# Feed-forward low parts moved from GpSimd to VectorE, adaLN halves replanned, bias copies spread: a two-layer hybrid diffusion backbone in float32

## The reference, cut to what matters

```python
for i in range(2):
    ml = adaln_terms(c[:, None, :], ada_w[i], ada_b[i])      # 9 terms of 1024: silu(c) @ ada_w + ada_b
    mc = adaln_terms(c_ctx, ada_w[i], ada_b[i])
    h = h + 0.5 * ml[2] * swiglu(modulate(h, norm_g[i, 0], ml[0], ml[1]), ffn_w_up[i, 0], ffn_w_down[i, 0])
    u = modulate(h, norm_g[i, 1], ml[3], ml[4])
    y = mixer(u)                                             # ends in an output projection
    h = h + ml[5] * y
    h = h + 0.5 * ml[8] * swiglu(modulate(h, norm_g[i, 2], ml[6], ml[7]), ffn_w_up[i, 1], ffn_w_down[i, 1])
    # hc (context) likewise, except that it is not needed after layer 1's mixer
return rmsnorm(h, final_norm_g)
```

## Time and profile before

| | before |
|---|---|
| median of 3 executions | 3018.96 us (3016.99 to 3019.55) |
| the profiled execution, its own time | 3020.68 us |
| its span, first to last instruction | 3018.9 us |
| PE busy | 2851.4 us (94%) |
| PE weight loads busy | 2653.7 us (88%) |
| DVE busy | 2255.8 us (75%) |
| ACT busy | 1255.2 us (42%) |
| POOL busy | 645.8 us (21%) |
| granted PE clock, mean | 0.984 of full |

### The profile page before, as it was taken

The page is one execution under the profiler, slowest core; times in us unless marked ns, Lnnn a source line. Parts: engine busy times, 40 slices in busy tenths (PEclk is TensorE's granted clock), DMA queues, the critical chain, the costliest instruction groups (busy, mean ns, idle before and its releaser), DMA issues.

```text
span 3018.9 us, 48480 instructions
## 1 busy us (share of the span) xinstructions
PE 2851.4 (94%) x18175; PEld 2653.7 (88%) x18175; DVE 2255.8 (75%) x3813; ACT 1255.2 (42%) x2458; POOL 645.8 (21%) x508
## 2 busy tenths in 40 slices
PE   8699999999999998988999999999999989999998
PEld 8689988999988886888999999889999877888887
DVE  7988888885546657398877787888888456498676
ACT  4234323543454456323433354333334336535444
POOL 1211011133332215221011113101111234431112
PEclk9899999999999999999999999999999999999999
DMA  6234444323320022232333322243332210223332
GB/s 251 85 100 130 117 131 137 90 80 119 127 79 15 8 75 79 70 104 68 104 116 126 116 88 64 64 132 123 132 126 82 89 36 2 78 72 103 98 88 81
DMA packets 160965, 285.49 MB, mean 95 GB/s; under 512 B 44078, under 2 KB 65502, under 8 KB 160606
## 3 DMA queue, kind: packets, MB, share of 16 engines
q1 hardware_dynamic: 157998, 275.99, 29.1%
q10 hardware_dynamic: 2736, 6.40, 0.5%
HBM read 270.73 MB, written 15.10 MB: 95 GB/s over the span
## 4 chain that ended last, share of the span: by engine, by line
PE 70%; DVE 16%; issue 5%; ACT 4%; SPq 2%; DMA 1%; POOL 1%; DVEq 0%; ACTq 0%; POOLq 0%
PE psum L2307 33%; PE psum L2322 26%; DVE ada_product L2005 2%; PE psum L2529 2%; DVE stats L1812 1%; SPq L999 1%; PE psum L2612 1%; DVE o_acc L2136 1%; DVE held L1812 1%; PE psum L2635 1%; DVE h L2266 1%; DVE wl L1788 1%; PE psum L2622 1%; PE psum L2514 1%; DVE sq L1694 1%
## 5 line engine op out<-in xcount | busy, mean ns | idle before, releaser
L1153 POOL TENSOR_TENSOR wl<-raw,wh 128x512 fp32r<-128x512 f32 (+3 forms) x278 | 477.8, 1719 | 2018.0 <-ACT wh L1247 2011.0
L1247 ACT ACTIVATE wh<-raw 128x512 fp32r<-128x512 f32 (+2 forms) x713 | 462.3, 665 | 556.6 <-DVE raw L1768 295.3
L2307 PE MATMUL psum<-uh,wh 128*128 128x256 f32 (+5 forms) x1552 | 399.8, 339 | 32.4 <-DVE h L2266 11.6
L2307 PE MATMUL psum<-uh,wl 128*128 128x256 f32 (+5 forms) x1552 | 395.5, 336 | 0.0
L2307 PE MATMUL psum<-ul,wh 128*128 128x256 f32 (+5 forms) x1552 | 395.1, 336 | 0.0
L2005 DVE SCALAR_TENSOR_TENSOR ada_product<-ada_w,cb 128x1024 f32<-128x1024 f32 x256 | 346.2, 1352 | 21.7 <-DMA ada_w<-in_ada_w 14.4
L2266 DVE SCALAR_TENSOR_TENSOR h<-psum,mod,h 128x512 f32<-128x512 f32 x360 | 215.0, 632 | 191.7 <-PE psum L2307 191.3
L2307 PE MATMUL psum<-ah,wh 128*128 128x512 f32 (+4 forms) x1040 | 304.6, 356 | 46.7 <-DVE h L2266 15.7
L1788 DVE TENSOR_TENSOR wl<-raw,wh 128x512 fp32r<-128x512 f32 x432 | 300.9, 697 | 51.3 <-ACT wh L1247 45.7
L2307 PEld LDWEIGHTS psum<-uh,wh 128*128 128x128 f32 (+1 forms) x1552 | 257.0, 190 | 59.2 <-DVE h L2266 14.7
L2307 PE MATMUL psum<-al,wh 128*128 128x512 f32 (+4 forms) x1040 | 298.3, 350 | 0.0
(11 more groups left out here) (324 smaller groups left out, 5137.2 us busy)
## 6 DMA issues: line engine op xcount, KB each, us to landing
raw<-in_w SPq DMA_DIRECT2D x448, 256.0 KB, 2.7
ada_w<-in_ada_w SPq DMA_DIRECT2D x128, 512.0 KB, 3.8
raw<-in_w SPq DMA_DIRECT2D x88, 512.0 KB, 3.7
spill<-cacc ACTq DMA_DIRECT2D x16, 384.0 KB, 2.4
scale_w<-in_scale_w SPq DMA_DIRECT2D x8, 512.0 KB, 14.6
raw<-in_w SPq DMA_DIRECT2D x32, 128.0 KB, 2.4
ada_w<-bias_final SPq DMA_DIRECT2D x16, 256.0 KB, 3.1
ada_start<-in_ada_w SPq DMA_DIRECT2D x7, 512.0 KB, 15.7
```

Source lines behind the costliest of these rows:

```text
L1153: nc.gpsimd.tensor_tensor(weight_tile(x, wl), raw_tile(slot_of[x]), weight_tile(x, wh).bitcast(f32), ALU.subtract).then_inc(lo_split, 1)
L1247: nc.scalar.activation(weight_tile(x, wh), src, ACT.Copy).then_inc(hi_split, 1)
L2307: ins = nc.tensor.matmul(bank, wt[:, k * w:(k + 1) * w], xt[:, k, cols], start=first, stop=last)
```

## The change

Four things change.

1. DVE makes the low parts of all gate, up and down units except the first three of (0,0), and those of the output projections' items 2 to 7, in `weight_lows(i)`, which takes the place of `pair_lows(i)` and goes through all its units in product order. POOL keeps the low parts of proj and of items 0 and 1 of each output projection.
2. The plan: term 8 of each layer goes over the eight items of the output projection before block 2. The first part of (0,1) has none any more. In later parts the downs of part 1 (two chunks) have no share; 84 shares carry 80 halves in (0,0) and 64 in (0,1) and (1,0).
3. SP issues two bias copies at each quarter product and each down from chunk 10's P1 on, instead of eight at P1 and P2.
4. At the first item of an output projection SP waits until the attention's maxima are done (unit 15 in layer 0, the last unit, 55, in layer 1) before it goes on to that item's loads; and the masks' load waits for the halves planned before it instead of for all.

The rest (`parts_of`, `classic_part`, `makes`, `t_made`, `u_made`) rewrites constants as functions with the same values. The diff, cut:

```diff
+def classic_part(x):
+    return 0
+def classic_pairs(x):
+    return sum(parts_of(x)[:classic_part(x) + 1])
...
     def shares(x):
         if x[0] == "down":
-            return 2 if x[3] + 1 < len(PARTS) else 0
+            full = x[3] + 1 < len(PARTS) and parts_of(x)[x[3]] == HALF_K
+            return 2 if full and x[3] != classic_part(x) else 0
+        if x[3] <= classic_part(x):
+            return 1 if x[3] else 0
         return {"P7": 1, "P5": 1}.get(x[0], 0)
...
+    def outs(layer):
+        return [i for i, x in enumerate(items) if x[:2] == ("out", layer)]
     over(ahead_of_downs(0, 0)[FUSED:], ada_chunks(0, [2]))
-    over(later_parts(0, 0), ada_chunks(0, range(3, 8)))
-    over(ahead_of_downs(0, 1), ada_chunks(0, [8]))
-    over(later_parts(0, 1), ada_chunks(1, range(4)))
-    over(later_parts(1, 0), ada_chunks(1, range(4, N_MOD)))
+    over(spread_out(0, 0), ada_chunks(0, range(3, 8)))
+    over(outs(0), ada_chunks(0, [8]))
+    over(spread_out(0, 1), ada_chunks(1, range(4)))
+    over(spread_out(1, 0), ada_chunks(1, range(4, 8)))
+    over(outs(1), ada_chunks(1, [8]))
...
+    vector_lows = [x for x, _, _, _ in units[FUSED:] if x[0] in ("gate", "up", "down") + PAIR or (x[0] == "out" and x[2] >= 2)]
...
             for x in items:
+                if x[:1] + x[2:] == ("out", 0):
+                    sp.wait_ge(max_done, 2 * (16 if x[1] == 0 else 56))
                 load_ada(number[x] if x[0] == "norm" and norm_no[x] else number[x] - ADA_LAG)
...
-                    elif windows and x[5] >= 10:
-                        if x[5] == 10 and not second:
-                            sp.wait_ge(table_made, 16 * 16)
-                        for wnd in windows[:8]:
-                            window(*wnd)
-                        windows = windows[8:]
+                    elif x[5] == 10 and not second:
+                        sp.wait_ge(table_made, 16 * 16)
+                        windows_due = windows
+                if x[0] in PAIR + ("down",) and x[1:3] == (0, 0):
+                    for wnd in windows_due[:2]:
+                        window(*wnd)
+                    windows_due = windows_due[2:]
...
-                    sp.wait_ge(ada_summed, on_dve(len(ada_order)))
+                    sp.wait_ge(ada_summed, on_dve(ADA_FIRST + sum(not v for i, c in plan.items() if i < number[x] for _, v in c)))
...
                     x, n, _, _ = units[done[0]]
-                    if x in low_no:
+                    if x not in vector_lows:
                         pool.wait_ge(lo_split, low_no[x])
...
-            def pair_lows(i):
-                while low_done[0] < len(pair_units) and issued(unit_of[pair_units[low_done[0]]], i):
-                    x = pair_units[low_done[0]]
-                    for y in sums_ahead.get(low_done[0], []):
+            def weight_lows(i):
+                while low_done[0] < len(vector_lows) and issued(unit_of[vector_lows[low_done[0]]], i):
+                    x = vector_lows[low_done[0]]
+                    for y in sums_ahead.get(x, []):
                         quarter_sum(y)
+                    if x in low_no:
+                        dve.wait_ge(lo_split, low_no[x])
                     dve.wait_ge(hi_split, unit_of[x] + 1)
-                    nc.vector.tensor_tensor(weight_tile(x, wl), pair_weight(x), weight_tile(x, wh).bitcast(f32),
-                                            ALU.subtract).then_inc(pair_lo, 1)
+                    src, done = (raw_tile(slot_of[x]), lo_split) if x in low_no else (pair_weight(x), pair_lo)
+                    nc.vector.tensor_tensor(weight_tile(x, wl), src, weight_tile(x, wh).bitcast(f32),
+                                            ALU.subtract).then_inc(done, 1)
```

More of the change, by code:

```diff
@@ L15 @@
 PARTS = [4, 2, 4, 4, 4, 4]
-CLASSIC = 4
+FIRST_PARTS = PARTS
 HALF_K = KD // 2
 QUARTER = HALF_K * P
-T_STEPS = 7 * HALF_K
 EPS = 1e-6
@@ L52, in segments, with parts_of @@
     return [LAT] if (layer, f) == (DEPTH - 1, 1) else [LAT, CTX]
+def parts_of(x):
+    return FIRST_PARTS if x[1:3] == (0, 0) else PARTS
+def classic_part(x):
+    return 0
+def classic_pairs(x):
+    return sum(parts_of(x)[:classic_part(x) + 1])
 def ffn_products(layer, f):
     items = []
-    chunks = [(layer, f, part, c, sum(PARTS[:part]) + c) for part, n in enumerate(PARTS) for c in range(n)]
-    for part, n in enumerate(PARTS):
+    parts, classic = (of(("", layer, f)) for of in (parts_of, classic_pairs))
+    chunks = [(layer, f, part, c, sum(parts[:part]) + c) for part, n in enumerate(parts) for c in range(n)]
+    for part, n in enumerate(parts):
         for key in [x for x in chunks if x[2] == part]:
             j = key[-1]
-            if j < CLASSIC:
+            if j < classic:
                 items += [("gate",) + key, ("up",) + key]
                 continue
-            if j == CLASSIC:
+            if j == classic:
                 items += [("P1",) + key, ("P2",) + key]
@@ L91, in shares, with within, spread_out @@
         if x[0] == "down":
-            return 2 if x[3] + 1 < len(PARTS) else 0
+            full = x[3] + 1 < len(PARTS) and parts_of(x)[x[3]] == HALF_K
+            return 2 if full and x[3] != classic_part(x) else 0
+        if x[3] <= classic_part(x):
+            return 1 if x[3] else 0
         return {"P7": 1, "P5": 1}.get(x[0], 0)
-    kinds = ("gate", "up", "down") + PAIR
+    def within(layer, f):
+        return [i for i, x in enumerate(items) if x[0] in ("gate", "up", "down") + PAIR and x[1:3] == (layer, f)]
     def ahead_of_downs(layer, f):
-        at = [i for i, x in enumerate(items) if x[0] in kinds and x[1:3] == (layer, f)]
+        at = within(layer, f)
         return at[:next(k for k, i in enumerate(at) if items[i][0] == "down")]
-    def later_parts(layer, f):
-        at = [i for i, x in enumerate(items) if x[0] in kinds and x[1:3] == (layer, f) and x[3]]
-        return [i for i in at for _ in range(shares(items[i]))]
+    def spread_out(layer, f):
+        return [i for i in within(layer, f) for _ in range(shares(items[i]))]
+    def outs(layer):
+        return [i for i, x in enumerate(items) if x[:2] == ("out", layer)]
     over(ahead_of_downs(0, 0)[FUSED:], ada_chunks(0, [2]))
-    over(later_parts(0, 0), ada_chunks(0, range(3, 8)))
-    over(ahead_of_downs(0, 1), ada_chunks(0, [8]))
-    over(later_parts(0, 1), ada_chunks(1, range(4)))
-    over(later_parts(1, 0), ada_chunks(1, range(4, N_MOD)))
+    over(spread_out(0, 0), ada_chunks(0, range(3, 8)))
[3 more added lines that the diff above has]
+    over(outs(1), ada_chunks(1, [8]))
     return plan
@@ L233, in weight_slots @@
         elif x[0] == "down":
-            out.append((x, PARTS[x[3]], P))
+            out.append((x, parts_of(x)[x[3]], P))
     return out
@@ L561, in down_at, with makes, t_start, t_made @@
             return x[4] if x[3] else FIRST_DOWNS.index(x[4])
+        def makes(x):
+            return 1
+        def t_start(x):
+            ffns = sorted({y[1:3] for y in items if y[0] == "P1"})
+            return sum((5 + 2 * makes(("P1",) + f)) * HALF_K for f in ffns if f < x[1:3])
+        def t_made(x, j):
+            return t_start(x) + (4 + makes(x)) * j
+        def u_made(x, j):
+            return t_made(x, HALF_K) + (1 + makes(x)) * j
         def segs_of(x):
@@ L907, in build @@
             for f in range(2):
-                at = lambda kind, j: (kind, layer, f, 0, j, j)
-                downs = [("down", layer, f, 0, i) for i in FIRST_DOWNS]
+                part = classic_part(("", layer, f))
+                at = lambda kind, j: (kind, layer, f, part, j, sum(parts_of(("", layer, f))[:part]) + j)
+                downs = [("down", layer, f, part, i) for i in FIRST_DOWNS]
                 if (layer, f) == (0, 0):
@@ L1301, in u_highs @@
             def u_highs(x, j):
-                act.wait_ge(t_added, T_STEPS * ffn_no(x) + 5 * HALF_K + 2 * j + 2)
-                act.wait_ge(product_done, number[("down",) + x[1:3] + (0, 0)])
+                act.wait_ge(t_added, u_made(x, j + 1))
+                act.wait_ge(product_done, number[("down",) + x[1:3] + (classic_part(x), 0)])
                 cols = slice(halves(x)[0].start, TU)
@@ L1496, in _ @@
                     t_highs(x, T_HIGHS[x])
-                if x[0] == "down" and x[3] == 0 and down_at(x) < HALF_K:
+                if x[0] == "down" and x[3] == classic_part(x) and down_at(x) < HALF_K:
                     u_highs(x, down_at(x))
@@ L1817, in t_sums @@
             def t_sums(x, j):
-                n = T_STEPS * ffn_no(x) + 5 * j + 1
+                n = t_made(x, j) + makes(x)
                 (ua, ub), (va, vb) = ([t[:, cols] for cols in halves(x)] for t in uv[j % 2])
@@ L2085, in _ @@
                     gated_low(low_at[x])
-                if x[0] == "down" and x[3] == 0:
+                if x[0] == "down" and x[3] == classic_part(x):
                     if x in T_LOWS:
@@ L2453, in _ @@
                             first_downs(x, [y for y in items[i + 1:i + 3] if begun(y)])
```

(2 more changed lines are left out.)

26 lines of the change are left out of this document (14 added, 12 removed).

## The result

| | before | changed |
|---|---|---|
| median | 3019.14 us (3016.99 to 3019.55) | 2969.14 us (2967.10 to 2969.84) |
| ratio | | 0.9835, 95% interval 0.9818 to 0.9852 |
| span of the profiled execution | 3018.9 us | 2965.3 us |
| PE busy | 2851.4 us | 2836.7 us |
| DVE busy | 2255.8 us | 2268.1 us |

What follows compares the result with a forecast made beforehand. PE was taken as the bound in general, DVE in block starts and where part 1 passes into 2. Terms summed to -28.4 us, taking the profiled 3020.7 to 2992.3, median 2991 us; range 2974 to 3011.

Steps and rivals of the forecast that it cites:

- Downs of part 1: Where part 1 passes into part 2: without adaLN halves the holes of 5.2, 3.0 and 5.2 us vanish, -13.4 us (-13.4 to -7).
- Bias copies: In (0,0): copies no longer in one burst before an adaLN load, so PE's lost 7.6 us return, -7 us (-7.6 to -3).
- denser adaLN plan: Parts 2 to 4 of (0,0): 80 halves on 84 shares instead of 100 load DVE more, +2 us (0 to +12).
- Start of (0,0): DVE bounds it: 11 to 13 us of POOL's blocking go, 10.5 us of low parts come, net -1 us (-6 to +6).
- about even: At small parts: some 0.7 us of POOL's 1.47 us per low part hits DVE, and 0.70 us of DVE work replaces it.
- (1,1), parts 1 to 5: PE's waits for low parts at the downs, 5.6 and 2.4 us, should halve: -4 us (-7 to +1).
- Half of the 8.0: Parts 1 to 5 of (1,1): PE's 5.6 us waiting for activation and 2.4 for weight low parts, half of which should go.
- Layer 1's projection and the start behind it: DVE needs 7.1 us a product against steps of 5.58; the start of (1,1) wins back 2.9: net +9 us (+2 to +15).
- Start of (0,1): 16 adaLN halves leave it: -17.6 us, and +1.8 for low parts made in order, so -15.8 us (-18 to -8).
- start of (1,0): DVE in order makes a low part at 20.3 us where PE wants it at 18.2: +1.8 us (0 to +6).
- Rival A: DVE becomes the bound in ordinary parts: up to 67 us slower; at 3 us a part 3027 us; chance 0.10.
- Rival C: More comes back from POOL's blocking in (0,0)'s start, (1,1) and layer 1's projection: 2991 - 15 = 2976 us; chance 0.14.

Runs made afterwards that it cites:

- the copies' run: The changed kernel with the bias table's copies in bursts of eight in front of the quarter products again: 2982.89 us, its four times between 2976.69 and 2986.63.

## Why the prediction was right in direction and wrong in size

The forecast's sum misses 25.4 us of the profiled difference of 53.8. The steps, in its own terms:

- **Downs of part 1: -13.4 forecast, -20.6 measured.** The cause was right and is shown (the passages stay at 76.2 with the low parts on POOL). The failed step is that the holes' length was taken as the gain. The rows already had the rest: the clock of 0.95 in two of those stretches was not priced. Those two passages lost 2.9 us each in PE's busy time beside their holes, about half of it at half clock. That of (0,1) lost 1.3 at a full clock, so the clock isn't all of the price.
- **Bias copies: -7 forecast, -10.7 measured**, the same step: 7.7 us of holes (the earlier trace rows had 7.6) and 3.0 beside them, half of these behind the one hole where the clock fell. The denser adaLN plan, forecast at +2, cost nothing; PE has no hole there.
- **Start of (0,0): -1 forecast, -6.1 measured.** The balance "about even" failed. DVE took on 10.8 us of low parts (12.9 less 2.1) and its busy time fell by 3.8, so POOL's 25.75 us had cost it 14.6. I counted from 67.2 us on only, where POOL shows 20.7, and so left out 5 us of POOL's work in front. The stage gained 2.3 us more than DVE; no run isolates that, and 1.6 of it lie within the stage's scatter.
- **(1,1), parts 1 to 5: -4 forecast, -6.7 measured.** PE's waits for `al` fell from 5.6 us to 2.4, those for `wl` from 2.4 to none. "Half of the 8.0" was too little in this execution: 5.6 of them went. With the scatter of this stage (-3.4 to -6.7 in kernels with the same instructions there) the miss is not clear of noise.
- **Layer 1's projection and the start behind it: +9 forecast, +5.7 measured.** The mechanism is right: PE waits for DVE's `wl`, and the step is 6.6 us. But the forecast had 7.1, and from the first step on, where the first two still take 5.6; and an adaLN half takes 1.22 us there, not the 1.35 that was priced. DVE's rstd comes 7.8 us later instead of 11.6 (whose terms, 10.8 + 2.7 + 1.2 + 0.35 - 2, give 13.1), and 2.1 us are won back behind it instead of 2.9. Kernels with the same instructions there had +6.1 to +8.2, so most of this miss is within the scatter. Moving the halves costs 8.6 by itself. The low parts give 2.2 back without the halves, and 10.4 with them (367.5 to 357.1); that they are worth more where DVE is fuller was not in the sum.
- **Start of (0,1): -15.8, measured -16.5; start of (1,0): +1.8, measured +2.1.** The first came out because it was read from a whole stage of the same work, clock included, and not from holes; the second as worked out, with the hole where `up` 1 waits for its low part (20.3 less 18.2 gives the 2.1; the forecast put 1.8). That DVE is busy nearly throughout in all the stages with holes was misread for the starts of (1,0) and (1,1), 87.8 of 99.5 us and 70.3 of 79.6: in the start of (1,0) the late low part counted, not DVE's load.
- **Rival A** did not occur: DVE is busy 78.5 us of 92.7. It was near enough, though: 24 extra low parts at 24 products in a row, 16.6 us of work, made DVE the bound (7.9 us of holes, 8.7 covered). **Rival C**, the nearest, named POOL's hold only and was still 7 us short of the result.

The largest single step that failed is the price of a hole: 7.2 us on the passages and 3.0 behind the copies' holes were left out, and no bound allowed for them, since none went beyond the hole's own length ("-13.4 to -7", "-7.6 to -3"), though that was no upper end of the gain. The balance of POOL's hold against DVE's low parts is the second (5.1 us in the start of (0,0)); the bounds there, -6 and -7, just about held it. What stays open: which holes the half clock follows, and why the copies' run scattered by 10 us.

## What to carry to other kernels

Price a hole of the matrix engine by the stage's length against the same matmuls without the hole, not by the hole's own length. Where that can't be read, take 0.3 us beside each hole where the granted clock stays full and about 2 us where it falls, and look at the granted clock of the stretch first. Work on GpSimd is not free for VectorE: here 0.5 to 0.7 of POOL's time came out of DVE's, whether DVE was full or had 9 us free. The stage got longer by it only where DVE was full, so move the work to VectorE in full stages; elsewhere it may stay on GpSimd. Gains of two edits that relieve the same engine in the same stage don't add.

## What the runs showed of the hardware that was not expected

- In two passages of the kernel before, 3.4 us at half clock came behind five holes of 0.3 to 1.8 us; in another kernel the same passage had 6.7 us of such holes and kept the full clock. A single hole of 2.2 us was followed by half clock, one of 3.0 us was not. Nine holes of 0.5 to 2.4 us in one part, with half clock five times, cost 10.1 us beyond their 14.0.
- The cost of a POOL low part to DVE depends on what DVE does: an instruction reading PSUM stayed at 745 ns beside any load of POOL, while small ones with two SBUF inputs more than doubled (478 ns without POOL, 1126 with POOL's low parts made twice; 128x256), as these two rows of the start of (0,0) have it, the changed kernel and the run with POOL's work doubled:

```profile
L1862 DVE SCALAR_TENSOR_TENSOR stats<-h,mod,rstd 128x256 f32<-128x256 f32 x8 | 3.8, 478 | 0.0
```

```profile
L1870 DVE SCALAR_TENSOR_TENSOR stats<-h,mod,rstd 128x256 f32<-128x256 f32 x8 | 9.0, 1126 | 0.0
```
